# The first product quad of the FFN: the rounding of its seven weight blocks moves from GpSimd to ScalarE

## The reference

```python
f = rms_norm(h, ffn_pre_norm[i])
f = (jax.nn.silu(f @ w_gate[i]) * (f @ w_up[i])) @ w_down[i]
h = h + rms_norm(f, ffn_post_norm[i])
```

## Time and profile before

| | us |
|---|---|
| median of 3 runs | 1817.67 |
| lowest and highest | 1817.55, 1818.24 |
| profiled execution, its own time | 1816.68 |
| its span, first to last instruction | 1814.9 |
| TensorE busy in the span | 1793.3 (99%) |
| VectorE, GpSimd, ScalarE busy | 1402.8, 1079.3, 688.3 |

### The profile page before, as it was taken

One profiled execution on the slowest core, in us unless ns is written; L12 is line 12 of the kernel. 1 busy time (PEld: TensorE's weight loads), 2 busy tenths in 40 slices (PEclk: granted clock), 3 DMA queues, 4 the chain that ended last, 5 costly groups with the idle time before them and its releaser, 6 DMA issues.

```text
span 1814.9 us, 22572 instructions
## 1 busy us (share of the span) xinstructions
PE 1793.3 (99%) x8522; PEld 1500.0 (83%) x8522; DVE 1402.8 (77%) x1612; ACT 688.3 (38%) x1204; POOL 1079.3 (59%) x750
## 2 busy tenths in 40 slices
PE   9999999999999999999999999999999999999998
PEld 8888888888888888888888888888888888888887
DVE  7879866666596757666599989668888875698897
ACT  5555577853321111111143334415433343333313
POOL 3056632170259988888778877632655455567554
PEclk9999999999999999999999999999999999999999
DMA  6342310042313323143375631113332231943222
GB/s 162 92 155 56 114 44 17 18 129 93 106 46 105 116 81 116 59 151 116 104 268 184 232 128 47 47 47 115 117 116 105 105 139 71 358 175 106 75 99 93
DMA packets 126577, 204.44 MB, mean 113 GB/s; under 512 B 31987, under 2 KB 87923, under 8 KB 123012
## 3 DMA queue, kind: packets, MB, share of 16 engines
q1 hardware_dynamic: 126434, 202.93, 33.0%
q10 hardware_dynamic: 34, 0.07, 0.0%
HBM read 149.42 MB, written 53.04 MB: 112 GB/s over the span
## 4 chain that ended last, share of the span: by engine, by line
PE 70%; DVE 5%; POOL 2%; issue 2%; ACT 1%; DMA 0%; DVEq 0%; SPq 0%; POOLq 0%
PE ps L1333 62%; PE ps L1660 1%; PE ps L1662 1%; PE ps L1661 1%; POOL ring_lo L1189 1%; POOL ring_hi L1188 1%; DVE y L3534 1%; PE ps L1898 1%; PE ps L1899 1%; PE ps L1900 1%; DVE y L3527 0%; PE ps L1775 0%; DVE xs_lo L3361 0%; PE ps L1539 0%; PE ps L1647 0%
## 5 line engine op out<-in xcount | busy, mean ns | idle before, releaser
L1333 PE MATMUL ps<-f_hi,ring_hi 128*128 128x512 f32 x384 | 149.7, 390 | 1.3 <-POOL ring_lo L1189 1.3
L1333 PE MATMUL ps<-f_hi,ring_lo 128*128 128x512 f32 x384 | 149.4, 389 | 0.0
L1333 PE MATMUL ps<-f_lo,ring_hi 128*128 128x512 f32 x384 | 149.4, 389 | 0.0
L1267 POOL TENSOR_TENSOR ring_lo<-w_sum,ring_hi 128x512 fp32r<-128x512 f32 x60 | 93.1, 1563 | 51.8 <-ACT ring_hi L2459 51.7
L1189 POOL TENSOR_TENSOR ring_lo<-w_sum,ring_hi 128x512 fp32r<-128x512 f32 x80 | 118.0, 1475 | 6.7
L1333 PE MATMUL ps<-d_w_hi,d_hid_hi 128*128 128x512 f32 x312 | 121.5, 390 | 0.3 <-DVE hid L3227 0.3
L1333 PE MATMUL ps<-d_w_lo,d_hid_hi 128*128 128x512 f32 x312 | 121.4, 389 | 0.0
L1333 PE MATMUL ps<-d_w_hi,d_hid_lo 128*128 128x512 f32 x312 | 121.4, 389 | 0.0
L2332 ACT ACTIVATE f_copy<-ps 128x512 f32<-128x512 f32 x60 | 35.4, 597 | 220.9 <-PE ps L1333 201.9
L1333 PE MATMUL ps<-xs_hi,ring_hi 128*128 128x512 f32 x256 | 100.0, 391 | 1.4 <-DVE xs_lo L3361 1.4
L1333 PE MATMUL ps<-xs_hi,ring_lo 128*128 128x512 f32 x256 | 99.6, 389 | 0.0
(11 more groups left out here) (546 smaller groups left out, 5796.4 us busy)
## 6 DMA issues: line engine op xcount, KB each, us to landing
d_raw<-hid_rows SPq DMA_DIRECT2D x37, 512.0 KB, 4.4
stage<-in_w_up SPq DMA_DIRECT2D x22, 512.0 KB, 4.4
wd_raw<-in_w_down SPq DMA_DIRECT2D x22, 512.0 KB, 5.2
raw_w<-in_w_gate SPq DMA_DIRECT2D x20, 512.0 KB, 4.8
stage<-in_pool_w_in SPq DMA_DIRECT2D x16, 512.0 KB, 4.9
raw_w<-in_pool_w_in SPq DMA_DIRECT2D x16, 512.0 KB, 4.7
m_rows<-u_row SPq DMA_DIRECT2D x16, 512.0 KB, 2.6
z_rows<-z_buf SPq DMA_DIRECT2D x8, 1024.0 KB, 4.1
```

The lines of the kernel that those rows point to most:

```text
L1267: g.tensor_tensor(as_blocks(lo, src), src, as_blocks(hi, src).bitcast(F32), ALU.subtract).then_inc(w_split, 1)
L1333: last = mm(out_ap, l, r, start=(start and j == 0), stop=(stop and j == n - 1), skip_group_check=onto)
```

## The change

For quad 0 alone, the seven roundings leave GpSimd's queue and go to ScalarE's, behind the rounding of the last factor (line 2327 before) and ahead of the first f_copy. ScalarE takes over the waits for the weights, for the sums and for the slots, and counts w_hi_ready; GpSimd waits for that count block by block and subtracts. The later users of w_hi_ready count from a base that is seven higher. block_source moves to where both engines' programs can call it.

```diff
@@ -432,6 +432,7 @@
         IN_QUADS = 6
         POS_LANDED = 16 * (5 + 16)
         IN_BLOCKS, IN_SUMS, IN_COPIES, IN_LANDED = 7 * IN_QUADS, 4 * IN_QUADS, 3 * IN_QUADS, 16 * IN_QUADS
+        IN_HI = IN_BLOCKS + 7
         US_SUMS, US_PARTS, US_ROWS = 16, 4, 0
         US_ORDER = (1, 0, 2, 3)
 
@@ -572,6 +573,12 @@
             return raw_w[r][:, k, :].rearrange("p (k n) -> p k n", k=4)[:, :, c * P:(c + 1) * P]
 
         SUM_OF, SUM_AT = {2: 0, 1: 1, 3: 2, 5: 3}, {1: 2, 3: 3, 5: 4}
+
+        def block_source(r, o):
+
+            if o in (0, 4, 6):
+                return wblock(r + 2, o // 6, 0 if o == 0 else 1)
+            return w_sum[r][:, SUM_OF[o], :]
 
         def as_blocks(x, like):
 
@@ -1199,11 +1206,6 @@
             pool.wait_ge(raw_in[0], IN_LANDED + raw_landed(1))
             whole_blocks(1, 4)
 
-            def block_source(t, r, o):
-                if o in (0, 4, 6):
-                    return wblock(r + 2, o // 6, 0 if o == 0 else 1)
-                return w_sum[r][:, SUM_OF[o], :]
-
             def product_blocks(t, r, slots_free):
                 pool.wait_ge(raw_in[1 - r], IN_LANDED + raw_landed(2 + r) + 32 * ((t - 2 - r) // 2))
                 for o in range(7):
@@ -1211,14 +1213,18 @@
                         pool.wait_ge(w_summed, IN_SUMS + 4 * (t - 2) + SUM_AT[o])
                     if o in (0, 1, 3, 5):
                         slots_free(min(o + 1, 6) if o else 0)
-                    split_block(o, block_source(t, r, o))
-
-            def std_slots_free(o):
-                pool.wait_ge(std_full, {0: 3, 2: 4, 4: 7, 6: 8}[o])
+                    split_block(o, block_source(r, o))
+
+            def first_block_lo(o):
+                src = block_source(0, o)
+                hi, lo = ring[o]
+                pool.wait_ge(w_hi_ready, IN_BLOCKS + o + 1)
+                g.tensor_tensor(as_blocks(lo, src), src, as_blocks(hi, src).bitcast(F32), ALU.subtract).then_inc(w_split, 1)
 
             pool.wait_ge(fs_hi_ready, US_PARTS + 12)
             g.tensor_tensor(f_sum[2][1][:], f_raw[2][:], f_sum[2][0][:].bitcast(F32), ALU.subtract).then_inc(fs_split, 1)
-            product_blocks(2, 0, std_slots_free)
+            for o in range(7):
+                first_block_lo(o)
             product_blocks(3, 1, lambda o: pool.wait_ge(prod_full, IN_BLOCKS + o + 1))
             for i in range(2, FG):
                 for r in range(2):
@@ -1226,7 +1232,7 @@
 
             for s in range(N_DOWN):
                 src, (hi, lo) = w_down_block(s), d_w[s % 4]
-                pool.wait_ge(w_hi_ready, IN_BLOCKS + s + 1)
+                pool.wait_ge(w_hi_ready, IN_HI + s + 1)
                 g.tensor_tensor(lo[:], src[:], hi[:].bitcast(F32), ALU.subtract).then_inc(w_split, 1)
                 if not d_split_by_dve(s):
                     src, (hi, lo) = d_raw[s % 6], d_hid[s % 4]
@@ -1263,7 +1269,7 @@
             def pool_block_lo(q, o):
                 src = pool_block(q, o)
                 hi, lo = ring[o]
-                pool.wait_ge(w_hi_ready, IN_BLOCKS + block_hi(q, o))
+                pool.wait_ge(w_hi_ready, IN_HI + block_hi(q, o))
                 g.tensor_tensor(as_blocks(lo, src), src, as_blocks(hi, src).bitcast(F32), ALU.subtract).then_inc(w_split, 1)
 
             for o in FIRST_ORDER:
@@ -1276,7 +1282,7 @@
                     pool_block_lo(q, o)
             def out_weight_lo(i, o):
                 src, (hi, lo) = w_out_block(o), d_w[(7 * i + o) % 4]
-                pool.wait_ge(w_hi_ready, IN_BLOCKS + HI_W + 7 * i + o + 1)
+                pool.wait_ge(w_hi_ready, IN_HI + HI_W + 7 * i + o + 1)
                 g.tensor_tensor(lo[:], src[:], hi[:].bitcast(F32), ALU.subtract).then_inc(w_split, 1)
 
             def out_rows_lo(i, o):
@@ -2326,6 +2332,15 @@
             act.wait_ge(std_full, 6)
             f(f_sum[3][0][:], f_raw[3][:], ACT.Copy).then_inc(fs_hi_ready, 1)
 
+            act.wait_ge(raw_in[1], IN_LANDED + raw_landed(2))
+            for o in range(7):
+                if o in SUM_AT:
+                    act.wait_ge(w_summed, IN_SUMS + SUM_AT[o])
+                if o in (0, 1, 3, 5):
+                    act.wait_ge(std_full, (3, 4, 0, 7, 0, 8)[o])
+                src = block_source(0, o)
+                f(as_blocks(ring[o][0], src), src, ACT.Copy).then_inc(w_hi_ready, 1)
+
             def copy_product(q, bank0, copies, j):
                 o = (0, 2, 3)[j]
                 act.wait_ge(prod_full, IN_BLOCKS + quad_full(q, o))
```

## The result

| | before | changed |
|---|---|---|
| median, us | 1817.66 (9 runs) | 1822.33 (9 runs) |
| lowest to highest | 1817.17 to 1818.24 | 1819.16 to 1823.25 |
| ratio, 95% interval | | 1.0025 [1.0016, 1.0033] |

The changed kernel is slower by 4.7 us, 0.25%. The forecast was +2.1 us with a range up to 1821.3, so the sign was right and the size too small by more than half. One execution of a kernel further down (1992.9 us, at a mean clock of 0.851) stood in a slower state of the chip and is left out of its comparison.

The account below looks back on a forecast made before the run. TensorE, busy 99% of 1814.9 us, was taken as the bound. A 3.3 us wait ahead of block 4 instead of 1.2 gave +2.1 on the 1817.67 us median: 1819.8 us, main case 1819.0 to 1821.0, range 1816.3 to 1821.3.

Parts of the forecast that it names:

- What bounds it, and who is late next: TensorE, 99% busy; in quad 0, block 4 waits for GpSimd's subtraction, next for f_copy behind VectorE's line 3137.
- The stall on ring_lo: TensorE's wait ahead of block 4 in quad 0, for GpSimd's subtraction: 1.19 us lost, forecast to go.
- The turns of VectorE and GpSimd: Quad 0: strict turns with only long subtractions end VectorE's line 3093 at 545.35 and line 3137 at 549.4, 3.3 us later.
- The size of the gap term: Ahead of block 4 in quad 0: TensorE waits 3.3 us instead of 1.2, +2.1 us.
- Work taken as free: ScalarE's seven copies (4.3 us, in its idle time), GpSimd's added waits and the shifted weight loads cost nothing.
- about when they did: The next sums, behind the next weights' loads, were forecast to start about as before, at 557.97.
- The clock falls: Rival: the gap ahead of block 4 lowers TensorE's clock, costing 1.5 to 3 us: 1821.3 to 1822.8; chance 0.10.
- It decides from the gap's length: In the clock rival: the length of the 3.3 us gap ahead of block 4 decides whether TensorE's clock falls.
- a bare +2.1: Main case: only the longer wait ahead of block 4 costs time, 1819.8 us (1819.0 to 1821.0); chance 0.62.

Follow-up runs that it names:

- The kernel with the short turns given back: The changed kernel, but GpSimd rounds each block of quad 0 again behind ScalarE before it subtracts: 1817.92 us, ratio 1.0001.

## Why the prediction was wrong: its waits came as forecast, its clock did not

**What bounds it, and who is late next.** Right. The stall on ring_lo went, f_copy took its place, and the factor subtraction releases it.

**The turns of VectorE and GpSimd.** Right to 0.1 us at each end that was forecast. The kernel with the short turns given back confirms the cause from the other side. The rule of the Trainium skill, SBUF — State Buffer, section Who interferes with whom, that one of the two waits until the other's instruction is done, holds here: 1.78 us for a sum whose own turn is 0.54.

**The size of the gap term.** +2.1 forecast, +2.35 measured, since TensorE was ready 0.1 us sooner (the 48 matmuls of blocks 0 to 3 started over 10.65 us in place of 10.78) and block 4 started 0.1 later than forecast.

**Work taken as free.** Right for ScalarE's seven copies (done at 539.46, twelve microseconds ahead of f_copy), for the added waits, and for the loads in what they cost: their issue follows the stores at once (552.92 and 553.78), with no wait of TensorE behind them. The next sums did not begin "about when they did": with the 2.28 taken off they begin at 559.83 against 557.97, inside the slack.

**The clock.** This is the step that failed: "The clock falls ... Chance 0.10", "It decides from the gap's length". That the clock would fall behind the gap, and at what price (1.5 to 3 us, 1821.3 to 1822.8; measured 1.6 and 2.8 us, median 1822.3), was right; its chance was not. In 17 of 21 executions the mean clock reads 0.998 or less, so the kind that I forecast, a bare +2.1, is the rare one (1819.1 to 1819.2 twice, 1820.3, and the profiled 1821.2 with its late start), and the range ended at 1821.3 where this rival began. I took a clean 1.04 us gap in the trace as evidence for a gap three times as long, and nothing in the trace spoke for gaps of that length; a wait of 1.90 us at 12.92, with a clock of 1.00 behind it, I had set aside with the first 13 us. No row was there to set the chance by; then it is near one half and belongs in the range. Nor does the gap's length decide: at 3.4 us four of 21 kept their clock. Two terms of the price had no row either. The transposes of the earlier trace rows read 1.00 on both sides, so they do not show the lower level (0.43 against 0.227 us at a granted 0.50 do), and no row gave the length of a low stretch, which took 3.40 us of TensorE's work in one trace and 5.98 in another. The Trainium skill, TensorE: Matmul & The Clock Gate, section HAM oscillation, says that a long enough idle gap brings the clock back to its lower level. The runs agree, and show it as a share and not as a bound: 17 of 21 at 3.4 us, 6 of 11 at 2.8, 2 of 11 at 1.8.

**The first 525 us.** The profile after has 2.3 us there that the change cannot reach. They are scatter: 1.0 us is there at the first product (13.91 against 12.92), 1.5 at 253 us and 2.3 at 424, all ahead of the changed work, and what sets it is left open. The last transposes of the f_blk rows begin at 496.7 us in the profile before, at 499.0 in the one after, and between 497.0 and 498.5 in the ten traces of the experiments, with or without the change. Two single profiles are not to be subtracted from end to end; each stage is to be read against its own beginning.

## What to carry to other kernels

Where two engines take turns instruction by instruction, the late engine's time is its own work and, for each of its instructions, one turn of the other: taking the short instructions off one engine makes the other wait for the long ones each time, and work may get slower by getting less. Before an early release is counted as a gain, look for the next condition of the same wait (here f_copy, 1.2 us sooner), and trace it back through the turns that its engine takes with another. A wait of TensorE that grows past 1 us has to be priced with what its clock does behind it, which here cost as much again as the longer wait.

## What the runs showed of the hardware

TensorE's clock can fall behind a gap of 1.84 us (at 13 us, one of twelve traces) or 2.79 us (quad 0), and not in every execution. The share of executions that read 0.998 or less grows with the gap in quad 0: 0 of 65 at 1.0 us, 2 of 11 at 1.8, 6 of 11 at 2.8, 7 of 11 at 3.0, 17 of 21 at 3.4; with 11 executions each, neighbours in this row are not told apart. It can be low already when work comes back (2.79 us and one of 3.38 us), or fall 1.5 us later in the midst of dense matmuls (3.35 us). Two sizes of loss were traced, 1.6 and 2.8 us. The mean granted clock of an execution (0.998 or 0.997 on 1820 us) tells how much was lost, though not where, while a busy share of 99% shows nothing.

In quad 0, before and after, GpSimd's operations (with one operand as with two) and VectorE's operations with two operands in SBUF took turns, one instruction of each, for as long as both had work: GpSimd held for 0.48 or 1.15 us, VectorE for 0.54 or 2.14. VectorE's operations that read PSUM took no part (two in 1.27 us).
